# Sums of squares of three norm halves moved from TensorE to VectorE, in a two-block transformer kernel

## The reference

```python
def layer_norm(x, g, b):
    mu = jnp.mean(xf, -1, keepdims=True)
    var = jnp.mean(jnp.square(xf - mu), -1, keepdims=True)
    return (xf - mu) * lax.rsqrt(var + EPS) * g + b

def _rmsnorm(x, g):
    return x * rsqrt(mean(x * x) + eps) * g
...
x = layer_norm(alpha * x + gate * (mixed @ w_out), ln1_g, ln1_b)        # first norm
x = layer_norm(alpha * x + gate * (relu(h @ w_ff1) ** 2 @ w_ff2), ...)  # second norm
h = _rmsnorm(x, e_norm) * (1 + scale) + shift                           # even norm
p = h @ e_w_in                                                          # even projection
```

## Time and profile before

| | |
|---|---|
| median of 3 runs | 2692.74 us (2689.59 to 2699.69) |
| the profiled execution's own time | 2691.15 us |
| its span, first to last instruction | 2689.3 us |
| mean granted TensorE clock | 0.966 |
| PE busy | 2496.9 us (93%) |
| DVE busy | 1397.6 us (52%) |
| ACT busy | 610.2 us (23%) |
| POOL busy | 732.4 us (27%) |

### The profile page before, as it was taken

How to read it: one execution, slowest core, us unless ns; L and a number is a source line. 1 busy time by engine, 2 the same in 40 slices (tenths; PEclk the granted TensorE clock), 3 DMA queues, 4 the chain that set the end, 5 groups by cost and what they waited for, 6 DMA issues and landing times.

```text
span 2689.3 us, 29003 instructions
## 1 busy us (share of the span) xinstructions
PE 2496.9 (93%) x11544; PEld 1946.7 (72%) x11544; DVE 1397.6 (52%) x1577; ACT 610.2 (23%) x882; POOL 732.4 (27%) x490
## 2 busy tenths in 40 slices
PE   5998779989999999999998689999998999999998
PEld 3876556657678888888886468886586778878877
DVE  7556743434643444444435779996528321336633
ACT  3002224431422001101123421113204210023311
POOL 1241320015462332332345211210045223340011
PEclk9999879999999999999999899999999999999999
DMA  6651000022232332332222121112232531110021
GB/s 225 200 162 61 20 18 8 8 95 86 59 106 83 95 98 75 94 98 88 80 84 80 38 94 42 34 39 102 70 122 82 160 78 47 47 40 1 1 86 71
DMA packets 228851, 206.96 MB, mean 77 GB/s; under 512 B 15248, under 2 KB 203280, under 8 KB 227712
## 3 DMA queue, kind: packets, MB, share of 16 engines
q1 hardware_dynamic: 223552, 178.61, 22.0%
q10 hardware_dynamic: 3840, 21.89, 2.1%
q0 software_dynamic: 1344, 4.91, 0.5%
HBM read 180.35 MB, written 17.83 MB: 74 GB/s over the span
## 4 chain that ended last, share of the span: by engine, by line
PE 79%; DVE 10%; issue 3%; ACT 3%; PEld 2%; POOL 1%; DMA 1%; PEldq 1%; ACTq 0%; DVEq 0%; SPq 0%; POOLq 0%
PE G L1633 28%; PE G L304 26%; PE M L3001 3%; PE G L1099 2%; PE M L307 2%; DVE WPT L3038 2%; PE G L2506 1%; PE M L2986 1%; PE M L400 1%; PE M L1649 1%; PE G L2322 1%; PE M L2322 1%; PE M L1010 1%; PE G L2349 1%; PE M L2508 1%
## 5 line engine op out<-in xcount | busy, mean ns | idle before, releaser
L278 POOL TENSOR_SCALAR WH<-RAW 128x1024 fp32r<-128x1024 f32 (+1 forms) x154 | 132.7, 861 | 888.4 <-PE G L1633 516.2
L304 PE MATMUL G<-HH,WH 128*128 128x512 f32 x1056 | 337.3, 400 | 14.7 <-POOL WL L2164 7.8
L304 PE MATMUL G<-HH,WL 128*128 128x512 f32 x1056 | 332.9, 396 | 0.0
L304 PE MATMUL G<-HL,WH 128*128 128x512 f32 x1056 | 332.8, 396 | 0.0
L281 POOL TENSOR_TENSOR WL<-RAW,WH 128x1024 fp32r<-128x1024 f32 (+1 forms) x154 | 299.4, 1944 | 12.9
L1633 PE MATMUL G<-HH,WH 128*128 128x512 f32 x640 | 227.2, 404 | 13.5 <-POOL WL L281 8.7
L304 PEld LDWEIGHTS G<-HH,WH 128*128 128x128 f32 x1056 | 188.6, 189 | 61.6 <-issue 19.5
L1633 PE MATMUL G<-HH,WL 128*128 128x512 f32 x640 | 223.7, 398 | 0.0
L1633 PE MATMUL G<-HL,WH 128*128 128x512 f32 x640 | 223.7, 398 | 0.0
L304 PEld LDWEIGHTS G<-HL,WH 128*128 128x128 f32 x1056 | 188.8, 188 | 42.4
L304 PEld LDWEIGHTS G<-HH,WL 128*128 128x128 f32 x1056 | 188.9, 188 | 42.2
(11 more groups left out here) (536 smaller groups left out, 4430.5 us busy)
## 6 DMA issues: line engine op xcount, KB each, us to landing
RAW<-in_w_ff SPq DMA_DIRECT2D x40, 512.0 KB, 3.9
RAW<-in_w_ff SPq DMA_DIRECT2D x80, 256.0 KB, 2.7
WVEC<-in_w_ada SPq DMA_DIRECT2D x24, 512.0 KB, 4.7
FVEC<-in_e_w_mod SPq DMA_DIRECT2D x24, 512.0 KB, 3.9
FVEC<-in_o_w_mod SPq DMA_DIRECT2D x24, 512.0 KB, 3.7
RAW<-in_o_w_in SPq DMA_DIRECT2D x24, 512.0 KB, 3.6
RAW<-in_e_w_in SPq DMA_DIRECT2D x20, 512.0 KB, 3.5
ADA<-in_w_ada SPq DMA_DIRECT2D x4, 2048.0 KB, 19.6
```

The source lines that it names most:

```text
L278: pool.tensor_scalar(hi, raw, 1.0, 0.0, ALU.mult, ALU.add).then_inc(w_high, 1)
L304: m = pe.matmul(G[s][:, n * w:(n + 1) * w], part[s][:, k, :], acts[i][:, k, n * w:(n + 1) * w], start=first, stop=last)
```

## The change

Seven edits:

1. In three of the four layer-norm halves (both of the first norm, the first of the second) VectorE adds up the squares in `HNR` as they come (`squares_add`, seven adds), and TensorE makes one product with ONES instead of eight. A square now waits for the add that has used its buffer. The second norm's second half keeps the eight products (`last_var_pe`).
2. The variance's product stands one unit later in TensorE's list, and so the even norm's first sum (`en_sum_pe`).
3. In the first norm's first half VectorE's adds stand in two pieces, behind the evictions of o(0,1,1) and o(0,2,1), and the eviction of o(0,3,1) moves ahead of the reciprocal.
4. In the first norm's second half ScalarE's root, and VectorE's reciprocal, move behind the feed of a(0,3,0).
5. Of the even norm's first half, the reciprocal moves behind the centring of the second norm's second half, and ScalarE's tiles are no longer one ahead of VectorE's low halves.
6. GpSimd alone splits units 2 and 3 of the even projection.
7. SWAPW is issued as the first of the three window tables.

```diff
         def norm_var_pe(pe, tag, h):
-            for f in range(KT):
-                pe.wait_ge(S(tag + "_sq"), KT * h + f + 1)
-                sq = (HSQ2 if tag == "l2" else HSQ)[f % 2]
-                pe.matmul(M[1][:, half(h)], ONES[:], sq[:], start=(f == 0), stop=(f == KT - 1))\
-                  .then_inc(S(tag + "_squ"), 1)
+            pe.wait_ge(S(tag + "_va"), 7 * h + 7)
+            pe.matmul(M[1][:, half(h)], ONES[:], HNR[h][:], start=True, stop=True).then_inc(S(tag + "_var"), 1)
...
-            after = {("o", 0, 0, 1): lambda: norm_mean_pe(pe, "l1", 0), ("o", 0, 2, 1): lambda: norm_var_pe(pe, "l1", 0),
-                     ("a", 0, 0, 0): lambda: norm_mean_pe(pe, "l1", 1), ("a", 0, 2, 0): lambda: norm_var_pe(pe, "l1", 1),
+            after = {("o", 0, 0, 1): lambda: norm_mean_pe(pe, "l1", 0), ("o", 0, 3, 1): lambda: norm_var_pe(pe, "l1", 0),
+                     ("a", 0, 0, 0): lambda: norm_mean_pe(pe, "l1", 1), ("a", 0, 3, 0): lambda: norm_var_pe(pe, "l1", 1),
...
-                     ("a", LAST, 2, 1): lambda: norm_var_pe(pe, "l2", 0),
-                     ("b", LAST, 4, 1): lambda: en_sum_pe(pe, 0)}
+                     ("a", LAST, 3, 1): lambda: norm_var_pe(pe, "l2", 0),
+                     ("b", LAST, 5, 1): lambda: en_sum_pe(pe, 0)}
...
             norm_mean_pe(pe, "l2", 1)
-            norm_var_pe(pe, "l2", 1)
+            last_var_pe(pe)
...
                     act.wait_ge(S(tag + "_c"), g + 1)
-                    if g >= 2:
-                        act.wait_ge(S(tag + "_squ"), g - 1)
+                    if h and f < 2:
+                        act.wait_ge(S(tag + "_va"), 6 + f)
+                    elif f >= 2 and tag == "l2" and h:
+                        act.wait_ge(S("l2_squ"), f - 1)
+                    elif f >= 2:
+                        act.wait_ge(S(tag + "_va"), 7 * h + max(f - 2, 1))
...
             feed(("a", 0, 2, 0))
+            feed(("a", 0, 3, 0))
             root("l1", 1)
-            feed(("a", 0, 3, 0))
...
             en_root(0)
-            en_tile(0, 0)
             squares("l2", 1)
-            en_tile(1, 0)
             root("l2", 1)
...
                 second_finish(f, 1)
-                if f + 2 < KT:
-                    en_tile(f + 2, 0)
+                en_tile(f, 0)
...
+            def squares_add(tag, a, b, h):
+                sq = HSQ2 if tag == "l2" else HSQ
+                for f in range(a, b):
+                    dve.wait_ge(S(tag + "_sq"), KT * h + f + 1)
+                    if f > 1:
+                        dve.wait_ge(S(tag + "_va"), 7 * h + f - 1)
+                    dve.tensor_tensor(HNR[h][:], sq[0][:] if f == 1 else HNR[h][:], sq[f % 2][:], ALU.add)\
+                       .then_inc(S(tag + "_va"), 1)
...
             center("l1", 1)
-            for j in (1, 2):
+            squares_add("l1", 1, KT, 1)
+            for j in range(1, 4):
                 feed_low(("a", 0, j, 0))
             inverse("l1", 1)
-            feed_low(("a", 0, 3, 0))
...
             center("l2", 0)
+            squares_add("l2", 1, KT, 0)
...
+            center("l2", 1)
             en_inverse(0)
-            evict_ff(("b", LAST, 6, 1))
-            gather_ff(6, 1)
             en_scaled(0, 0)
-            evict_ff(("b", LAST, 7, 1))
-            gather_ff(7, 1)
-            center("l2", 1)
+            inverse("l2", 1)
+            scaled("l2", 0, 1)
             en_scaled(1, 0)
             en_low(0, 0)
-            inverse("l2", 1)
-            scaled("l2", 0, 1)
-            en_scaled(2, 0)
-            en_low(1, 0)
             context_low()
             for f in range(1, KT):
                 scaled("l2", f, 1)
                 rms_add(f - 1, 1)
-                if f + 2 < KT:
-                    en_scaled(f + 2, 0)
                 if f + 1 < KT:
-                    en_low(f + 1, 0)
+                    en_scaled(f + 1, 0)
+                en_low(f, 0)
...
             for i in range(20):
                 r, U_ = r0 + i, u0 + i
-                if i < 2:
+                if i < 4:
                     split_one(pool, r, U_, KT)
                     continue
...
-                    for dst, src in ((WC, "cos_win"), (WS, "sin_win"), (SWAPW, "swap_win")):
+                    for dst, src in ((SWAPW, "swap_win"), (WC, "cos_win"), (WS, "sin_win")):
```

More of the change, by code:

```diff
@@ L1645, in norm_var_pe, with last_var_pe @@
         def norm_var_pe(pe, tag, h):
+            pe.wait_ge(S(tag + "_va"), 7 * h + 7)
+            pe.matmul(M[1][:, half(h)], ONES[:], HNR[h][:], start=True, stop=True).then_inc(S(tag + "_var"), 1)
+        def last_var_pe(pe):
             for f in range(KT):
-                pe.wait_ge(S(tag + "_sq"), KT * h + f + 1)
-                sq = (HSQ2 if tag == "l2" else HSQ)[f % 2]
-                pe.matmul(M[1][:, half(h)], ONES[:], sq[:], start=(f == 0), stop=(f == KT - 1))\
-                  .then_inc(S(tag + "_squ"), 1)
+                pe.wait_ge(S("l2_sq"), KT + f + 1)
+                pe.matmul(M[1][:, half(1)], ONES[:], HSQ2[f % 2][:], start=(f == 0), stop=(f == KT - 1))\
+                  .then_inc(S("l2_squ"), 1)
         def context_turn_pe(pe):
@@ L1711, in root @@
             def root(tag, h):
-                act.wait_ge(S(tag + "_squ"), KT * h + KT)
+                if tag == "l2" and h:
+                    act.wait_ge(S("l2_squ"), KT)
+                else:
+                    act.wait_ge(S(tag + "_var"), h + 1)
                 if h:
@@ L1919, in wf_dve @@
             center("l1", 0)
-            for f in (1, 2):
-                evict_out(f, 1)
-                gather_out(f, 1)
+            evict_out(1, 1)
+            gather_out(1, 1)
+            squares_add("l1", 1, 5, 0)
+            evict_out(2, 1)
+            gather_out(2, 1)
+            squares_add("l1", 5, KT, 0)
+            evict_out(3, 1)
+            gather_out(3, 1)
             inverse("l1", 0)
@@ L1927, in wf_dve @@
                 low(f - 1, 0)
-                if f in (1, 3, 5, 7):
-                    evict_out(3 + f // 2, 1)
-                    gather_out(3 + f // 2, 1)
+                if f % 2:
+                    evict_out(4 + f // 2, 1)
+                    gather_out(4 + f // 2, 1)
             low(KT - 1, 0)
-            evict_out(7, 1)
-            gather_out(7, 1)
             feed_low(("a", 0, 0, 0))
             center("l1", 1)
-            for j in (1, 2):
+            squares_add("l1", 1, KT, 1)
+            for j in range(1, 4):
                 feed_low(("a", 0, j, 0))
             inverse("l1", 1)
-            feed_low(("a", 0, 3, 0))
             scaled("l1", 0, 1)
@@ L2020, in wf_dve @@
             rms_add(KT - 1, 0)
-            evict_ff(("b", LAST, 4, 1))
-            gather_ff(4, 1)
-            evict_ff(("b", LAST, 5, 1))
-            gather_ff(5, 1)
+            for f in range(4, KT):
+                evict_ff(("b", LAST, f, 1))
+                gather_ff(f, 1)
+            center("l2", 1)
             en_inverse(0)
-            evict_ff(("b", LAST, 6, 1))
-            gather_ff(6, 1)
             en_scaled(0, 0)
-            evict_ff(("b", LAST, 7, 1))
-            gather_ff(7, 1)
-            center("l2", 1)
+            inverse("l2", 1)
+            scaled("l2", 0, 1)
             en_scaled(1, 0)
             en_low(0, 0)
-            inverse("l2", 1)
-            scaled("l2", 0, 1)
-            en_scaled(2, 0)
-            en_low(1, 0)
             context_low()
@@ L2148, in ein_high @@
             r, U_ = info("ein")["r0"] + i, info("ein")["u0"] + i
-            if 2 <= i < 20:
+            if 4 <= i < 20:
                 act.wait_ge(raw_loaded[r % 2], (r // 2) * 16 + 16)
@@ L2157, in ein_pool @@
                 r, U_ = r0 + i, u0 + i
-                if i < 2:
+                if i < 4:
                     split_one(pool, r, U_, KT)
                     continue
-                pool.wait_ge(ein_wh, i - 1)
+                pool.wait_ge(ein_wh, i - 3)
                 pool.sem_inc(w_high, 1)
```

## The result

The changed kernel takes 2700.99 us (median of 20 executions, 2695.52 to 2708.86); the kernel before, run beside it, 2693.34 us (20 executions, 2687.25 to 2699.69). The ratio is 1.0034, 95% interval 1.0026 to 1.0041: 9.1 us slower (7.0 to 11.0), inside the 0.5% that I had called no change, and inside the range.

What follows compares the result with a forecast made beforehand. TensorE's waits were taken to bound the kernel (79% of the span). Terms 3.7 + 2.3 + 0.8 - 1.0 + 1.7 + 1.5 - 4.9 - 0.5 = +3.6 us gave 2694.8, stated as 2695.5 us; range 2681 to 2704.

Steps and rivals of the forecast that it cites:

- First norm, first half, +3.7: Adds wait for GpSimd passes, TensorE stands 5.4 us for the variance; unit a(0,0,0) starts 3.7 us later.
- First norm, second half, +2.3 and +0.8: Late PSUM tile, low-clock a(0,3,0), root and reciprocal behind its feed: +2.3 us; wait at b(0,f,0) and half a clock drop: +0.8.
- Second norm, first half, -1.0: Same pattern as the first norm's second half, but the root already stood behind a(7,3,1): reciprocal 1.0 us sooner.
- Second norm, second half: Eight products kept; even norm's later sum brings the centring 10.8 us sooner and the reciprocal 12.8 us sooner, at 1502.0.
- Even norm, +14.4 from that reciprocal to the last add: Even-norm loop: turns of 4.2 us instead of 2.75, from a reciprocal at 1502.0 to the last add's end at 1542.0.
- the term of +1.7: Even norm's last add ends at 1542.0 against 1540.4; a separate +1.5 us was booked for last tile and sum at low clock.
- Even projection, -4.9: GpSimd splits units 2 and 3 early; the third unit waits only for ScalarE's eviction and starts 4.9 us sooner.
- Window tables, -0.5: With SWAPW first, WS lands last with the same bytes ahead; bounds 0 and -2.8 us, -0.5 taken.
- the port doesn't bite: Rival, chance 0.15: GpSimd's passes fall beside the adds, a half's seven take 5 us; kernel about 2680 us.
- The clock stays low: Rival, chance 0.10: new waits in the seven evictions and even norm's eight turns drop the clock, 1.8 us each; 2710 at eight.

Runs made afterwards that it cites:

- e5_psum: The changed kernel with squares 1 to 7 of the three halves written to PSUM, one SBUF input per add: 2685.93 us, ratio 0.9972 to the kernel before.
- e6_feed: The changed kernel with ScalarE's feed of a(0,1,0) and a(7,1,1) put between squares 1 and 2: 2690.61 us, ratio 0.9989 to the kernel before.
- e2_swap: The kernel before with only the window tables' order changed, SWAPW issued first: 2698.7 us, ratio 1.0005 to the kernel before.

## Why the prediction was right, and where its sizes were off

- **First norm, first half, +3.7:** +3.8 measured (703.76 - 698.80 - 1.15). The adds of up to 2.9 us, the wait of 5.4 (5.52 measured) and its cause came out; e5_psum shows the cause.
- **First norm, second half, +2.3 and +0.8:** +4.6 measured. The wait for the PSUM tile was there (5.14 from the end of a(0,2,0) to the start of a(0,3,0), where I had 4.6), but the unit behind it took 8.62 us and I had put 7.4, a unit that had spent less of itself at the low level. These two are 0.5 and 1.2 us; the rest of the path came out 0.2 shorter than forecast. The mechanism was right (e6_feed), its size was not.
- **Second norm, first half, -1.0:** -0.3 measured; the wait for the PSUM tile is again 0.5 us longer than I had put.
- **Second norm, second half:** the step that failed. I had its reciprocal 12.8 us sooner; against the middle it is 8.2 sooner. 1.2 of the 4.6 us are the mean's: it came at 1500.51, 8.4 sooner where I had 9.6, and why is not shown. The other 3.4 lie behind it: I let the time from mean to reciprocal shrink from 13.8 us to 10.5, and it stayed 13.9. Nearly all of that, 3.1 us, is the price of the eight products. The prediction doesn't name one, but it gives the reciprocal 2.0 us more than the centring ahead of it, which is what the products gain if they take 7.44 us, as in the first norm, and not the 9.44 of this place. They took 10.55, since their first 6.4 us ran at the low clock.
- **Even norm, +14.4 from that reciprocal to the last add:** 1554.38 - 1514.39 = 40.0 where I had 40.0. The turns of 4.20 us were exact. With the step ahead of it 4.6 too good, the term of +1.7 became +6.2; with the low clock at its end +8.1 (I had +3.2).
- **Even projection, -4.9:** -5.0 at the wait, -6.4 by the marks. The 1.5 us more go with less low clock behind the wait, which I had not counted.
- **Window tables, -0.5:** 0.2 in e2_swap, alone; 0.9 less wait in the changed kernel.
- **Of the rivals**, "the port doesn't bite" is out by the adds of the changed kernel, and e5_psum shows what it priced: the first norm gained 11.4 us there (from +8.4 to -3.0 by the marks; I had 9.3). "The clock stays low" was in part true, in the even norm's loop, at 41 us of low clock, but not through the seven evictions, where only a stretch from 748 to 751 us was low.

So of the two large errors, 4.6 and 1.7 us, 3.1 and 1.2 are of one kind: a TensorE price taken from a place with another share of low clock. Some luck hid part of them. The unchanged middle gave 1.8 us back, because one low-clock stretch near 910 us was half as long as before, which nothing in the prediction covers, and the even projection gave 1.5 more than forecast. Without these 3.3 us the median would stand at 2704.3, just outside the upper end of the range, 2704.
